# Attention: a head pair's products with V issued in one run instead of four visits

## What is computed

```python
# nsa_selected and nsa_window: 8 heads each, causal, 512 keys
s = einsum('bqgrd,bkgd->bgrqk', qb, kb) * ATTN_SCALE
p = safe_softmax(s, mask)
return einsum('bgrqk,bkgd->bqgrd', p, vb)
# fox_group: 8 heads, causal, with the forget-gate bias
s = einsum('bqhd,bshd->bhqs', qb, k) * ATTN_SCALE + cb[..., None] - c[:, :, None, :]
p = safe_softmax(s, mask)
return einsum('bhqs,bshd->bqhd', p, v)
```

## Time and profile before

| quantity | value |
|---|---|
| median of 3 runs | 483.23 us |
| lowest, highest | 481.22, 483.38 us |
| span of the profiled execution, first to last instruction | 480.1 us |
| busy TensorE (matmul) | 451.0 us, 94% of the span |
| busy TensorE (weight load) | 345.2 us, 72% |
| busy VectorE | 306.4 us, 64% |
| busy ScalarE | 250.3 us, 52% |
| busy GpSimd | 75.4 us, 16% |
| nsa attention, first to last V visit of the trace | 174.5 to 245.0 us |
| fox attention, the same | 351.7 to 386.8 us |

### The profile page before, as it was taken

One profiled execution on the slowest core, in us unless ns is written; L12 is line 12 of the kernel. 1 busy time (PEld: TensorE's weight loads), 2 busy tenths in 40 slices (PEclk: granted clock), 3 DMA queues, 4 the chain that ended last, 5 costly groups with the idle time before them and its releaser, 6 DMA issues.

```text
span 480.1 us, 6629 instructions
## 1 busy us (share of the span) xinstructions
PE 451.0 (94%) x2328; PEld 345.2 (72%) x2328; DVE 306.4 (64%) x560; ACT 250.3 (52%) x472; POOL 75.4 (16%) x121
## 2 busy tenths in 40 slices
PE   5899999999779889999999999999899996999997
PEld 1576787878668766666677897987776674888885
DVE  5977469887987876676428855758866357522204
ACT  5556684767365656766528855842565435312200
POOL 3012230000000155556300000000354200000000
PEclk9999999999979999999999999999799999899999
DMA  8732234431131200000011242552200001932004
GB/s 253 297 92 84 96 81 132 123 96 54 54 114 44 87 2 3 0 2 2 1 44 44 89 131 90 143 166 87 89 2 1 1 17 71 332 105 89 0 1 175
DMA packets 12960, 39.52 MB, mean 82 GB/s; under 512 B 1792, under 2 KB 2048, under 8 KB 12672
## 3 DMA queue, kind: packets, MB, share of 16 engines
q1 hardware_dynamic: 12928, 39.11, 25.4%
HBM read 32.81 MB, written 2.10 MB: 73 GB/s over the span
## 4 chain that ended last, share of the span: by engine, by line
PE 75%; DVE 14%; issue 4%; ACT 3%; POOL 1%; DMA 1%; SPq 0%; POOLq 0%; DVEq 0%; ACTq 0%
PE bank L1110 10%; PE bank L1112 10%; PE bank L1111 10%; PE bank L1224 6%; PE bank L1206 5%; PE bank L1324 5%; PE bank L1325 4%; PE bank L1326 4%; PE bank L1196 3%; PE bank L1197 3%; PE bank L1121 2%; DVE wl L767 2%; PE bank L1090 2%; PE bank L1140 2%; PE bank L1092 2%
## 5 line engine op out<-in xcount | busy, mean ns | idle before, releaser
L1110 PE MATMUL bank<-xh,wh 128*128 128x512 f32 (+1 forms) x264 | 111.9, 424 | 0.0
L1112 PE MATMUL bank<-xh,wl 128*128 128x512 f32 (+1 forms) x264 | 104.4, 395 | 0.0
L1111 PE MATMUL bank<-xl,wh 128*128 128x512 f32 (+1 forms) x264 | 103.8, 393 | 0.0
L767 DVE TENSOR_TENSOR wl<-raw,wh 128x1024 fp32r<-128x1024 f32 x51 | 62.0, 1220 | 33.9 <-ACT wh L502 33.5
L502 ACT ACTIVATE wh<-raw 128x1024 fp32r<-128x1024 f32 x51 | 53.2, 1050 | 35.1 <-PE bank L1326 34.5
L951 DVE TENSOR_REDUCE negmax<-bank 128x1 f32<-128x128 f32 (+3 forms) x96 | 46.0, 484 | 28.0 <-PE bank L1198 27.9
L1110 PEld LDWEIGHTS bank<-xh,wh 128*128 128x128 f32 (+1 forms) x264 | 49.7, 188 | 14.8 <-issue 4.7
L1111 PEld LDWEIGHTS bank<-xl,wh 128*128 128x128 f32 (+1 forms) x264 | 49.6, 188 | 14.4 <-issue 3.9
L1112 PEld LDWEIGHTS bank<-xh,wl 128*128 128x128 f32 (+1 forms) x264 | 49.5, 187 | 11.7
L470 POOL TENSOR_SCALAR probs<-probs,rcp,gates 128x128 f32<-128x128 f32 (+3 forms) x52 | 31.9, 622 | 126.5 <-DVE rcp L965 126.3
L610 ACT ACTIVATE probs<-bank,negmax 128x256 f32<-128x256 f32 (+3 forms) x77 | 40.6, 528 | 21.0 <-DVE negmax L951 19.9
(11 more groups left out here) (200 smaller groups left out, 790.1 us busy)
## 6 DMA issues: line engine op xcount, KB each, us to landing
raw<-in_w_in SPq DMA_DIRECT2D x39, 512.0 KB, 3.3
raw<-in_w_out SPq DMA_DIRECT2D x12, 512.0 KB, 3.7
x_raw<-in_xT SPq DMA_DIRECT2D x8, 256.0 KB, 6.4
x_res<-in_x_tok SPq DMA_DIRECT2D x1, 2048.0 KB, 8.3
out_y<-y_out SPq DMA_DIRECT2D x8, 256.0 KB, 2.1
cmp_w_sb<-in_cmp_w SPq DMA_DIRECT2D x1, 1024.0 KB, 9.8
kh_fox<-kh_fox SPq DMA_DIRECT2D x8, 128.0 KB, 2.4
kl_fox<-kl_fox SPq DMA_DIRECT2D x8, 128.0 KB, 2.5
```

Of the source, the lines that this page charges most:

```text
L767: dve.tensor_tensor(wl[:, c % HL, :], raw[:, c % RAW, :], wh[:, c % HL, :].bitcast(F32), ALU.subtract).then_inc(wl_ready, 1)
L1110: pe.matmul(dst, hi, xh[:, k, :], start=(k == 0), stop=False)
L1111: pe.matmul(dst, hi, xl[:, k, :], start=False, stop=False)
L1112: mm = pe.matmul(dst, lo, xh[:, k, :], start=False, stop=(k == KT - 1))
```

## The change

`values_step` now gives a pair only once, in what was the step of its first visit (step 5 of the next pair), and `pair_values` issues all four key tiles there, in the same order of key tile and head. `av_done` counts pairs instead of key tiles, and the three waits on it are rescaled. `finish_pair` still comes one step behind the last product, which is now step 6 and no longer step 12 (step 4 of the pair after that). No instruction that computes is added or removed.

```diff
--- before.py
+++ after.py
@@ -356,7 +356,7 @@
 
             w = u // PAIR_UNITS
             if w >= 2:
-                eng.wait_ge(av_done, NT * (w - 1))
+                eng.wait_ge(av_done, w - 1)
 
         def probs_of(u, a, b):
 
@@ -375,7 +375,7 @@
         def values_step(first, last, s):
 
             w, r = divmod(s - V_LAG - PAIR_UNITS, PAIR_UNITS)
-            return (w, r // 2) if r % 2 == 0 and first <= w * PAIR_UNITS < last else None
+            return w if r == 0 and first <= w * PAIR_UNITS < last else None
 
         block = ctx.enter_context(nc.Block())
 
@@ -926,7 +926,7 @@
                 group, i, b = pairs[w]
                 if b == 1:
                     return
-                dve.wait_ge(av_done, NT * (w + 1))
+                dve.wait_ge(av_done, w + 1)
                 o = OUT[out_of(w) % 2][:, :]
                 if group == "nsa":
                     if i == 0:
@@ -964,8 +964,8 @@
                             dve.wait_ge(p_scaled, 2 * (q - R_RING) + 2)
                         dve.reciprocal(rcp[:, q % R_RING, :], rsum[:, q % R_RING, :]).then_inc(rcp_ready, 1)
                     v = values_step(first, last, s - 1)
-                    if v is not None and v[1] == NT - 1:
-                        finish_pair(v[0])
+                    if v is not None:
+                        finish_pair(v)
 
 
             for k in range(KT):
@@ -1206,23 +1206,23 @@
                     mm = pe.transpose(PT[u % PTB][:, cols], probs_of(u, j * P, (j + 1) * P), ident)
                 mm.then_inc(pT_ready, 1)
 
-            def pair_values(w, j):
+            def pair_values(w):
 
                 group, i, b = pairs[w]
                 o = out_of(w)
-                if j == 0:
-                    for u in range(w * PAIR_UNITS, (w + 1) * PAIR_UNITS):
-                        wait_pT(pe, u)
-                    if b != 2:
-                        if o >= 2:
-                            pe.wait_ge(pair_done, o - 1)
-                        else:
-                            pe.wait_ge(cmp_o_read, NT - 1 + o)
-                for side in range(2):
-                    weights = pT[:, w % 2, side, 0:NT * KEYS].rearrange("p (t k) -> p t k", t=NT)
-                    moving = weights[:, j:NT, j * P:(j + 1) * P] if j < NT - 1 else pT[:, w % 2, side, PT_W - P:PT_W]
-                    mm = pe.matmul(OUT[o % 2][half_of(side), j * P:SEQ], values_of(w, side)[:, j, :], moving,
-                                   start=(b != 2 and j == 0), stop=(b != 1 and j == NT - 1))
+                for u in range(w * PAIR_UNITS, (w + 1) * PAIR_UNITS):
+                    wait_pT(pe, u)
+                if b != 2:
+                    if o >= 2:
+                        pe.wait_ge(pair_done, o - 1)
+                    else:
+                        pe.wait_ge(cmp_o_read, NT - 1 + o)
+                for j in range(NT):
+                    for side in range(2):
+                        weights = pT[:, w % 2, side, 0:NT * KEYS].rearrange("p (t k) -> p t k", t=NT)
+                        moving = weights[:, j:NT, j * P:(j + 1) * P] if j < NT - 1 else pT[:, w % 2, side, PT_W - P:PT_W]
+                        mm = pe.matmul(OUT[o % 2][half_of(side), j * P:SEQ], values_of(w, side)[:, j, :], moving,
+                                       start=(b != 2 and j == 0), stop=(b != 1 and j == NT - 1))
                 mm.then_inc(av_done, 1)
 
             def attention(first, last):
@@ -1238,7 +1238,7 @@
                         unit_transpose(s - T_LAG)
                     v = values_step(first, last, s)
                     if v is not None:
-                        pair_values(*v)
+                        pair_values(v)
 
 
             pe.wait_ge(ones_ready, 1)
```

## The result

| | before | changed |
|---|---|---|
| median | 482.51 us (4 runs) | 494.44 us (4 runs) |
| lowest, highest | 481.22, 483.38 | 492.46, 495.65 |
| ratio | 1 | 1.025 [1.0224, 1.0275] |
| span of the profiled execution | 480.1 us | 492.9 us |
| a full nsa pair, without and with `finish_pair` | 8.94 us | 10.00 and 10.31 us |

What follows compares the result with a forecast made beforehand. Attention was taken as bound nearly equally by TensorE's stream and a chain through VectorE and GpSimd. Per nsa pair +1.30 - 0.13 - 0 - 0.46 = +0.71 us; with finish_pair, tails and fox 8.2 us, giving 491.4 us, range 486.5 to 495.

Steps and rivals of the forecast that it cites:

- V to S6: TensorE, start of the value products to scores of unit 6: 2.31 us, so these scores come 1.30 later.
- V to T4: TensorE, start of the value products to transposes of unit 4: 5.05 us; the part behind the scores shortens by 0.13.
- V to T6: TensorE, start of the value products to transposes of unit 6: 7.16 us; unit 4 to unit 6 stays 2.11.
- T6 to T1': TensorE, transposes of unit 6 to those of the next pair's unit 1: 2.28 us, 0.46 gained, limited by ScalarE's copy.
- T1' to V': TensorE, transposes of the next pair's unit 1 to its value products: 0.21 us, taken as unchanged, no term in the sum.
- Taken like the others: First nsa pair, with the last recurrence output on VectorE: assumed to lose the same 0.71 us as other nsa pairs.
- closed chain: Transposes of unit 4 to those of unit 6, through VectorE and GpSimd: 2.11 us, claimed unchanged by the merge.
- slower rival: finish_pair costs its full 0.67 in six pairs and late units push the next pair's transposes: 494 to 496 us, chance 0.14.
- my own case: Main forecast for the whole kernel: 491.4 us, own range 488.9 to 493.9, chance 0.70.
- TensorE's stream deciding throughout: Rival: TensorE alone sets the pace, so the merge saves 8.4 to 9.9 us, giving 474 us; chance 0.07.
- Absorption: Rival: units in flight keep GpSimd fed during the long run; 478.6 us, or 485 if half absorbed; chance 0.09.
- V3: Fourth visit of value products in a pair, on TensorE before the next pair's unit 4 scores; removing it takes 0.50 out.

## Why the prediction was right, and by how much it was off

**What bounds the kernel.** Right. The full TensorE rows were no evidence of TensorE alone; with the reciprocal out of the chain the kernel before loses 0.08 a pair, so the two bounds lie that close. (The Trainium skill, Perfetto Trace Analysis, "Identifying the Most-Contended Engine", warns of matmul busy time. This case agrees: 451.0 us before, 449.5 after, in spans 12.8 us apart.)

**The terms of a nsa pair.**

| step | forecast | measured |
|---|---|---|
| V to S6 | 2.31 | 2.31 |
| V to T4 | 5.05 | 5.04 |
| V to T6 | 7.16 | 7.17 |
| T6 to T1' | 2.28 | 2.38 |
| T1' to V' | 0.21 | 0.44 to 0.53 |
| pair | 9.65 | 10.00 |
| pair with `finish_pair` | 9.91 | 10.31 |

The first three terms, on which the sign hung, were right to 0.01. The fourth has one hop mis-sized: I gave the end of ScalarE's copy to T1' 0.05, and it is 0.15. The fifth term was missing from the sum. I had taken T1' to V' as it was, though my own fourth term made T1' wait for ScalarE; whatever stands behind a late instruction is no longer hidden, and here eight semaphore waits stand there. Together 0.35 and 0.40 a pair, in five full pairs 1.9 us. The experiment with two waits gives 0.2 to 0.3 of it back.

**The first nsa pair.** "Taken like the others" was the other failed step: 12.21 against a forecast of 10.84, 1.4 us. The recurrence output on VectorE already made this pair 1.19 us longer than the others before; ahead of the closed chain it costs more, and the hole it makes brought the clock down. Moving it gives 10.10.

**finish_pair.** Forecast +0.26, measured +0.23 at T6. The other 0.09 between 10.00 and 10.31 lie between T1' and V' (0.44 and 0.53), and I don't put them down to it: with the recurrence output earlier the same pairs take 10.22 to 10.23, with 0.44 there. The part of the slower rival that gave it its full 0.67 in six pairs is refuted.

**Tails and fox.** nsa tail +0.71 (forecast 0.8), fox tail +0.87 (1.06), fox pairs +0.65 and +0.68 (0.67). No step failed; the fox tail was 0.2 over.

**The sum.** Inside nsa attention 5.84 forecast and 9.0 measured: 5.84 + 1.9 + 1.4 - 0.1 for the tail = 9.0. In fox 2.4 and 2.2. Inside attention 8.2 against 11.2, and 1.6 more in the span outside it. "All of it reaches the end" holds: from the last nsa V to the first fox scores it is 93.1 us in both kernels. The measured 494.4 is above the 488.9 to 493.9 that I gave my own case and inside the wider range up to 495, which took in a part of the slower rival; that it falls inside is owed to that width, not to the terms that I had left out. The 3.1 us outside the span were not a constant either: the changed kernel's profiled execution took 494.75 us with a span of 492.9, so 1.9; the rest of the 3.1 was most likely one execution against the median. It cancels in the difference.

**What I said the profile would show.** Idle time before T4 and T6 of 0.7 to 0.8 us each: measured 0.69 and 0.65, put down to GpSimd, right. T4 to T6 2.13 (2.36 with `finish_pair`): right. TensorE's busy time 8 to 10 us down: wrong, it is 1.5. I took the saving of 0.84 to 0.99 a pair, which is start-to-start time, for busy time; the rows of busy time did not contain most of it, and no run splits it further.

**The rivals.** TensorE's stream deciding throughout is refuted, and further off than I thought: even without the first chain the pair is 8.79, not 8.0, because of the copy of unit 3, a second chain that the forecast does not name. Absorption is refuted (T4 at 5.04). The slower rival's time, 494 to 496, fits the measured one by luck: neither of its two prices is there. `finish_pair` cost 0.2 to 0.3 and not 0.67, and in the full nsa pairs T2 and T3 come at 2.93 and 3.68, 0.62 and 1.37 behind S6 where they were 0.63 and 1.37 before, so they were not pushed.

## What to carry to other kernels

Short visits of one kind of work on an in-order engine may be filler for waits on other engines. Before merging them, ask of each one what the next instruction is waiting for: in this kernel, removing V3 gave time back (0.37 a pair), removing V1 and V2 from the place of a wait gave 0.14 and nothing, and putting all three in front of S6 delayed everything behind it by 1.30. When an instruction becomes late, price all that follows it on its queue as no longer hidden, semaphore waits too. And a repair that helps behind a late input (the reciprocal first) can cost time where the input is on time, so each belongs with its placement.

## What the runs showed of the hardware

- Eight semaphore waits (nine for b = 1 and in fox) in front of a TensorE instruction cost nothing while the engine is not held ahead of them (T1' to V 0.20). When the instruction ahead was itself released late, 0.44 to 0.53 us lie between the two; with six waits fewer it is 0.23. Six waits are thus 0.2 to 0.3 us. In fox the nine waits took 0.20 to 0.23 in the changed kernel, up to 0.36 in others. Why the same pair ends with 0.53 in one kernel and 0.44 in another stays open.
- In the changed kernel TensorE stood idle for 1.43 us ahead of T6 in the first nsa pair, after 0.69 ahead of T4 and 0.32 ahead of T5, and from 183.3 us on it ran 3.4 us at 1.2 GHz (granted clock 0.86 over the 12.21 us of that pair; 1.00 with 0.65 us of idle time in that place). In the four other kernels with such a hole there (1.42 to 2.15 us) the clock fell there, or just behind it, too. Waits of 0.64 to 0.70 us, two a pair over 40 us, left it at 1.00. The same instructions do not always fare alike: in the nsa tail, with waits of 0.98 and 0.95 us, the clock stayed at 2.4 GHz in the changed kernel's execution and fell for 3.4 us in that with two waits.
- The run of 16 products with V takes 2.30 to 2.31 us to the next instruction wherever it stands, at full clock, and the length of such a run says nothing of what it costs: 11.9 us over before in one place, 0.9 under it in another.
